# A two-block transformer kernel on one core: order of ScalarE's copies, source of the bias transfers, engine of the softmax scaling, and placement of half projections in its dilated attention

## The reference, cut to what matters

```python
q = rms(h @ w_q) * 64 ** -0.5                      # 3 groups x 16 heads x 64
for g, (window, dil) in enumerate(((128, 1), (512, 4), (2048, 16))):
    s = q_g @ k_g.T + bias_g                       # only distances <= window that dil divides
    ...
    lse = logsumexp(s); p = exp(s - lse); o_g = p @ v_g
wts = softmax(lse over the 3 groups)
o = sum_g wts_g * o_g
x = x + o @ w_o
```

## Time and profile before

| what | us |
|---|---|
| median of 3 runs (lowest to highest) | 2189.49 (2183.22 to 2194.12) |
| the profiled execution, as timed | 2188.71 |
| its span in the trace | 2186.9 |
| of this the dilated block, about | 1758 to 1984 |
| busy over the span: PE, DVE, ACT, POOL | 2013.5, 1170.5, 991.9, 501.5 |

### The profile page before, as it was taken

How to read it: one execution, slowest core, us unless ns; L and a number is a source line. 1 busy time by engine, 2 the same in 40 slices (tenths; PEclk the granted TensorE clock), 3 DMA queues, 4 the chain that set the end, 5 groups by cost and what they waited for, 6 DMA issues and landing times.

```text
span 2186.9 us, 36846 instructions
## 1 busy us (share of the span) xinstructions
PE 2013.5 (92%) x15863; PEld 1925.6 (88%) x15863; DVE 1170.5 (54%) x1389; ACT 991.9 (45%) x1157; POOL 501.5 (23%) x117
## 2 busy tenths in 40 slices
PE   7887999989899979999887999999999987879999
PEld 7875899988799979999886999899899986659998
DVE  5336577665577664437785633433444354556443
ACT  4325344355443453436333533476643455534433
POOL 1100122322022222230330123333222333001322
PEclk9867999999999999999888999999999999979999
DMA  7300345443245525555321455455455544324552
GB/s 263 136 17 1 116 156 192 168 164 135 97 155 193 191 97 193 175 190 183 117 78 58 159 187 173 160 174 167 144 181 189 176 162 151 101 63 151 177 187 102
DMA packets 57313, 321.13 MB, mean 147 GB/s; under 512 B 5693, under 2 KB 19124, under 8 KB 19828
## 3 DMA queue, kind: packets, MB, share of 16 engines
q1 hardware_dynamic: 42644, 304.49, 40.2%
q10 hardware_dynamic: 14560, 15.06, 2.3%
HBM read 318.41 MB, written 1.12 MB: 146 GB/s over the span
## 4 chain that ended last, share of the span: by engine, by line
PE 71%; issue 11%; DVE 10%; ACT 5%; DMA 1%; POOL 1%; ACTq 0%; SPq 0%; DVEq 0%; POOLq 0%
PE bank L371 22%; PE bank L372 22%; PE bank L373 22%; DVE lo L344 3%; ACT hi L338 1%; PE bank L429 1%; DVE xl L829 1%; PE bank L1502 1%; ACT arena L1663 1%; PE bank L466 1%; DMA arena<-rel_rows 1%; DVE arena L1577 1%; DVE arena L505 1%; POOL lo L344 1%; DVE arena L858 1%
## 5 line engine op out<-in xcount | busy, mean ns | idle before, releaser
L371 PE MATMUL bank<-xh,hi 128*128 128x256 f32 x3208 | 924.7, 288 | 37.4 <-DVE xl L829 20.2
L372 PE MATMUL bank<-xl,hi 128*128 128x256 f32 x3208 | 918.0, 286 | 0.0
L373 PE MATMUL bank<-xh,lo 128*128 128x256 f32 x3208 | 917.3, 286 | 0.0
L344 POOL TENSOR_TENSOR lo<-ring,hi 128x2048 fp32r<-128x2048 f32 x97 | 454.2, 4684 | 1548.3 <-ACT hi L338 1548.3
L338 ACT ACTIVATE hi<-ring 128x2048 fp32r<-128x2048 f32 x291 | 550.4, 1899 | 475.7 <-PE bank L373 471.0
L344 DVE TENSOR_TENSOR lo<-ring,hi 128x2048 fp32r<-128x2048 f32 x194 | 509.1, 2625 | 369.1 <-ACT hi L338 368.9
L371 PEld LDWEIGHTS bank<-xh,hi 128*128 128x128 f32 x3208 | 625.1, 195 | 50.4 <-issue 32.6
L372 PEld LDWEIGHTS bank<-xl,hi 128*128 128x128 f32 x3208 | 625.4, 195 | 0.6 <-issue 0.5
L373 PEld LDWEIGHTS bank<-xh,lo 128*128 128x128 f32 x3208 | 625.2, 195 | 0.2
L371 PE MATMUL bank<-gh,hi 128*128 128x256 f32 x1056 | 302.1, 286 | 16.5 <-DVE gl L765 15.7
L372 PE MATMUL bank<-gl,hi 128*128 128x256 f32 x1056 | 301.2, 285 | 0.0
(11 more groups left out here) (264 smaller groups left out, 1810.1 us busy)
## 6 DMA issues: line engine op xcount, KB each, us to landing
ring<-in_ffn_in SPq DMA_DIRECT2D x132, 1024.0 KB, 4.9
ring<-in_ffn_out SPq DMA_DIRECT2D x66, 1024.0 KB, 4.9
ring<-in_kv SPq DMA_DIRECT2D x24, 1024.0 KB, 4.8
ring<-in_hg_in SPq DMA_DIRECT2D x16, 1024.0 KB, 4.8
ring<-in_od_in SPq DMA_DIRECT2D x12, 1024.0 KB, 5.0
ring<-in_dq SPq DMA_DIRECT2D x12, 1024.0 KB, 4.8
ring<-in_ev_in SPq DMA_DIRECT2D x11, 1024.0 KB, 5.0
arena<-rel_rows ACTq DMA_DIRECT2D x16, 384.0 KB, 4.7
```

The source lines that it names most:

```text
L344: ns.tensor_tensor(lo[n % RING][:, 0:w], ring[n % RING][:, 0:w], hi[n % RING][:, 0:w].bitcast(F32), ALU.subtract).then_inc(lo_ok[lo_by[n]], 1)
L371: nc.tensor.matmul(out_, lh, rh, start=start, stop=False, **kw)
L372: nc.tensor.matmul(out_, lh, rl, start=False, stop=False, **kw)
L373: return nc.tensor.matmul(out_, ll, rh, start=False, stop=stop, **kw)
```

## The change

It has five parts, all in the dilated block, or in the helper `Soft` for this block alone:

1. ACT's order in `soft_act`: the hook with `squares` stands behind the copies of the turned blocks, no longer ahead of them.
2. The bias rows are issued by SP, in line with its loads: those of pair 0 behind the load of chunk 4, of pair 1 behind that of chunk 10, of pair 2 behind 11, of 3 behind 13, of 4 behind 14, of 5, 6 and 7 behind 15. Each still waits for the last addition of the unit before it.
3. The scaling of the exponentials is done by GpSimd (`soft_pool`). DVE keeps one reciprocal for each unit, which waits for the exponentials of both heads.
4. In return the low parts of chunks 5 to 11 move from GpSimd to DVE. GpSimd keeps chunks 1 and 3.
5. In rounds 0 to 4 the chunk `inside` is cut in two: its first half stands between the scores of the first and the second group, its second half between those of the second and the third.

```diff
             elif b == "dilated":
-                lo_by += ["V" if c in (0, 2, 4) or c >= 12 else "P" for c in range(len(streams[b]))]
+                lo_by += ["P" if c in (1, 3) else "V" for c in range(len(streams[b]))]
...
+        def scaled(s, u, e):
+            a, rr = s.att[u % s.nr][e], s.rr[:, 2 * (u % 4) + e, :]
+            return [(a[:, :, c0:c1], a[:, :, c0:c1], rr[:, r:r + 1].unsqueeze(2).broadcast_to([P, s.ns, c1 - c0]))
+                    for c0, c1, r in ((0, T, 3), (T, 384, 2))]
+
+        def soft_pool(pool, s):
+            for u in range(len(s.units)):
+                pool.wait_ge(*s.at("rec", u + 1))
+                for e in range(2):
+                    for out, exps, r in scaled(s, u, e):
+                        last = nc.gpsimd.tensor_tensor(out, exps, r, ALU.mult)
+                    last.then_inc(soft_sem["p"], 1)
...
             def weights(u):
...
-                for e in range(2):
-                    if not s.late:
-                        dve.wait_ge(*s.at("exp", 2 * u + e + 1))
-                        rec_step(nc.vector.reciprocal(both[:, e, 2:4], both[:, e, 0:2]))
-                    nc.vector.tensor_tensor(a[e][:, :, 0:T], a[e][:, :, 0:T],
-                                            both[:, e, 3:4].unsqueeze(2).broadcast_to([P, ns, T]), ALU.mult)
-                    nc.vector.tensor_tensor(a[e][:, :, T:384], a[e][:, :, T:384],
-                                            both[:, e, 2:3].unsqueeze(2).broadcast_to([P, ns, P]),
-                                            ALU.mult).then_inc(soft_sem["p"], 1)
+                dve.wait_ge(*s.at("exp", 2 * u + 2))
+                rec_step(nc.vector.reciprocal(both[:, :, 2:4], both[:, :, 0:2]))
...
+                if not s.by_pool:
+                    for e in range(2):
+                        for out, exps, r in scaled(s, u, e):
+                            last = nc.vector.tensor_tensor(out, exps, r, ALU.mult)
+                        last.then_inc(soft_sem["p"], 1)
...
                 if i in s.exps_first and 0 <= u < U:
                     exps(u)
-                s.hook(s.mid, "act", i, act)
+                if s.late:
+                    s.hook(s.mid, "act", i, act)
                 if j >= 0:
                     turned(j)
+                if not s.late:
+                    s.hook(s.mid, "act", i, act)
...
-            def biases_in(act, p):
+            def biases_in(sp, p):
                 if p >= 1:
-                    act.wait_ge(*soft.at("masked", 6 * p))
+                    sp.wait_ge(*soft.at("masked", 6 * p))
+                else:
+                    sp.wait_ge(rel_sent, 16)
+                    sp.wait_ge(lin, 1)
...
+            def sp_after(c):
+
+                return {4: [0], 10: [1], 11: [2], 13: [3], 14: [4], 15: [5, 6, 7]}.get(c, [])
...
-            soft.step = {(i, 2): lambda pe, c=c: project(pe, c) for i, c in inside.items()}
+            soft.step = {(i, h): half(c, h) for i, c in inside.items() for h in range(2)}
...
-            soft.after_exps = {p: lambda act, p=p: biases_in(act, p + 1) for p in range(7)}
...
+                        if b in parts and "sp" in parts[b]:
+                            parts[b]["sp"](sp, c)
```

More of the change, by code:

```diff
@@ L381, in build, with __init__ @@
         class Soft:
-            def __init__(self, units, ns, late, att, pt, nm, rr, copies, held=()):
+            def __init__(self, units, ns, late, att, pt, nm, rr, copies, held=(), by_pool=False):
+                self.by_pool = by_pool
                 self.units, self.ns, self.late, self.att, self.pt, self.nm, self.rr = units, ns, late, att, pt, nm, rr
@@ L389, in __init__ @@
                 self.after = {"pe": {}, "dve": {}, "act": {}}
-                self.turn_after, self.step, self.exps_first, self.after_exps = {}, {}, set(range(len(units) + 1)), {}
+                self.turn_after, self.step, self.exps_first = {}, {}, set(range(len(units) + 1))
                 n, pairs = len(units), 1 + max(un["pair"] for un in units)
@@ L396, in __init__ @@
                 adds = {"qk": n * ns, "masked": 2 * n * ns, "max": 2 * n, "exp": 2 * n,
-                        "rec": n * (1 if late else 2) + gates, "p": 2 * n, "turned": 2 * n * ns, "pt": 2 * n * ns,
+                        "rec": n + gates, "p": 2 * n, "turned": 2 * n * ns, "pt": 2 * n * ns,
                         "pv": n * ns, "oh": pairs - len(held), "o": pairs}
@@ L1914, in make_dilated @@
             N_HELD = 2
-            soft = Soft(units, 3, False, att, pt, NM, RR, copies, [DK[:, p, :] for p in range(N_HELD)])
+            soft = Soft(units, 3, False, att, pt, NM, RR, copies, [DK[:, p, :] for p in range(N_HELD)], True)
             inside = {0: 5, 1: 6, 2: 8, 3: 9, 4: 11}
@@ L1997, in biases_in, with sp_part @@
                         src = bass.AP(tensor=rel_rows.tensor, offset=(2 * p + e) * 1152 + u0, ap=[[1, P], [384, 3], [1, n]])
-                        act.dma_start(REL[e][:, :, lo:lo + n], src).then_inc(rel_in, 16)
+                        sp.dma_start(REL[e][:, :, lo:lo + n], src).then_inc(rel_in, 16)
+            def sp_after(c):
+                return {4: [0], 10: [1], 11: [2], 13: [3], 14: [4], 15: [5, 6, 7]}.get(c, [])
+            def sp_part(sp, c):
+                for p in sp_after(c):
+                    biases_in(sp, p)
             def dve_mid(i):
@@ L2066, in act_part @@
                 soft_act(act, soft)
-            return {"pe": pe_part, "dve": dve_part, "act": act_part}
+            return {"pe": pe_part, "dve": dve_part, "act": act_part, "sp": sp_part, "pool": lambda pool: soft_pool(pool, soft)}
         makers = {"even": make_even, "fox": make_fox, "hgrn": make_hgrn, "kv": make_kv, "dilated": make_dilated}
```

12 lines of the change are left out of this document (3 added, 9 removed).

## The result

The changed kernel takes 2208.05 us (median of 4 runs, 2204.8 to 2210.6), the kernel before 2187.66 us in the runs beside it. The ratio is 1.0081, with a 95% interval from 1.0058 to 1.0105: slower. (It is not the quotient of the two medians, which is 1.0093; so a difference told by ratios and one told by medians can be some 2 us apart.) The profiled execution took 2206.97 us with a span of 2205.2, which is 18.3 more than before. The whole difference stands behind the first scores of the dilated block. From the first scores of round 0 to the first turn of round 5 it was 108.15 us (1796.49 to 1904.64), and is 123.1 (1796.56 to 1919.65): +14.9. From that turn to the end it was 282.3, and is 285.55: +3.3.

What follows compares the result with a forecast made beforehand. PE, on 71% of the chain, was taken as the bound. 7.8 us up to round 5, 6.6 behind it and 5 of clock gave +19.4 on 2188.71, so 2208 us, range 2193 to 2222.

Steps and rivals of the forecast that it cites:

- a chain that was hidden is not any more: In rounds 0 to 4, additions, maxima and exponentials behind the third scores, 5.5 us, no longer run beside the chunk.
- The pause: In rounds 1 to 4 PE idles some 4.3 us in one piece behind the first turn, waiting for ACT's copy.
- Rounds 1 to 4: Rebuilt at 17.9 us each plus means, chunk and waits; against before: -3.7, +2.0, -0.4 and +3.4 us.
- three waits of the prediction: Round 1: 1.5 us for bias rows; round 2: 0.6 for the take-out and 0.5 for squares ahead of the means.
- The clock: Pauses in rounds 0 to 4 bring stretches at the lower clock level: 5 us taken, between none and 8.
- The tail: Behind round 5, turns wait for GpSimd's scaling, 4.5 us a unit against DVE's 3.0: +6.6 us in sum.
- The roots of round 4: Squares, high part and an output copy precede the roots, delaying round 5's turn: round 4 takes 24.1 us, +3.4.
- Bias rows: Pair 1's rows, issued by SP behind chunk 10's load, land around 1822, costing 1.5 us of wait in round 1.
- the faster one: Rival: waits between scores and late copies go, only GpSimd's 6.6 us is new: -12.7, 2176 us; chance 0.09.
- The cheap one: Rival, no change: chain exposed, but no slow stretch, GpSimd 3.0 us a unit, rows land in 4.8: 2197; chance 0.21.
- SP would be the bound: Rival, slower still: bias rows land 9.1 us after issue, scaling costs 5.3, pauses slow the clock: 2221 us; chance 0.14.
- the late copies: In four rounds the second turn waits for ACT's copies behind squares and a high part: 4 x 2.2 us saved.

Runs made afterwards that it cites:

- halves_0_2: Changed kernel with the inner chunk's second half behind the third scores instead of ahead of them; 2187.35 us, ratio to before 0.9988.
- filled: Changed kernel with matmuls whose results are never read put into PE's pauses in rounds 0 to 4; 2198.81 us, ratio to before 1.0052.
- dve_scales: Changed kernel with the scaling of the weights back on DVE; 2201.77 us, ratio to before 1.0063.
- whole_chunks: Changed kernel with the chunks of rounds 0 to 4 in one piece behind the third group's scores; 2188.25 us, ratio to before 1.0001.
- sp_bias_only: Kernel before with only the bias rows issued by SP, by the change's own table of loads; 2187.77 us, ratio to before 0.9995.
- late_on_vector: Changed kernel with whole chunks behind the third scores and units 5 to 7 scaled by DVE; 2183.46 us, ratio to before 0.9965.
- pool_scales_only: Kernel before with only GpSimd's scaling, one reciprocal a unit, and the low parts moved to DVE; 2198.80 us, ratio to before 1.0038.

## Why the prediction was right

It said 2208, in a range from 2193 to 2222, slower; 2208.05 was measured. The mechanism was the one named: a chain that was hidden is not any more. That the number fits to a microsecond is luck. The profiled execution moved by 18.3 us where 19.4 were said, and the terms behind it were off by more than that, in both directions. By its own steps:

- **The pause.** 4.3 us were foretold for rounds 1 to 4, and came as 4.39 three times, 5.19 in round 1. In round 0 the half of chunk 5 was to start near 1799.5 and did at 1799.10, the means near 1814.5 and did at 1814.21. From start to start round 0 took 21.8 us instead of 14.3, +7.5, where +6.5 was said.
- **Rounds 1 to 4.** Foretold 25.2, 21.8, 24.0 and 24.1 us before any clock; measured 26.0, 23.4, 26.75 and 25.1. Together they are 6.2 too long. PE worked at the lower level for 19.6 us in them, which at 44 to 50% is 8.6 to 9.8 us. So without the clock they were some 3 us shorter than foretold, and three waits of the prediction did not come: 1.5 for the bias rows in round 1, and in round 2 the 0.6 for the take-out and the 0.5 for the squares.
- **The clock.** The sum held 5 us for it, with 8 as the most. The slow stretches of rounds 0 to 4 cost 10 to 11 (22.5 us of work at the lower level). That hardly showed in the total, because the sum set rounds rebuilt at full clock against rounds of before that hold 4 us of slow clock themselves (8.6 us of work), and because the tail had less of it than before. Rounds 0 to 4 came out at +14.9; the prediction's 7.8 and 5 make 12.8. From before to after the clock took 6 to 7 us more in the rounds (halves_0_2 and filled point at 6 to 8), and 4 less in the tail. The term was right in kind, and it was the least founded: one stretch in the earlier trace rows, and a guess between none and 8.
- **The tail.** +6.6 was said and +3.3 measured (in dve_scales against the changed kernel it is 4.1 in the traces). 4.5 us a unit was right for units 6 and 7: 4.46, with 1.47 for the larger shape and 0.83 for the smaller. It was not for unit 5 (7.01), where the prediction had not looked at what DVE does beside it. The turns waited 5.70 + 1.31 and 6.56 + 1.31 us for GpSimd, where it had been 3.31 + 0.92 and 4.16 + 0.99 for DVE, 2.8 and 2.7 more; unit 5's 4.62 in place of 0.59 is 4.0 more. The two scores' waits of 1.22 came back. So the waits of PE did grow by 7.1 us, near the term. That the end moved by less is the clock: PE worked 18.5 us at the lower level there, where it had been 27.2 (3.4 of them behind the units, from 1985.9), which is 4 us less lost. The prediction had no such term.
- **The roots of round 4** were to end 5.5 us behind the last product. The turn that waits for them stood 1.53 us, and round 4 took 25.1 for the 24.1.
- **Bias rows.** The addition came at 1821.84, where 1822 was said. But the 1.5 us of wait that the prediction drew from it did not come: PE had no wait for a bank in round 1, and from the first scores to the second turn it took 14.88 us, against 14.74 in round 2. DVE had caught up before the third scores. Their lateness in round 3 did not show, since the exposed chain covers it: it does in whole_chunks.

Of the rivals, the faster one (the waits go and nothing replaces them) died of the point that the prediction named, the maxima that need all three groups. The cheap one (2197) left out 5 us of clock, 4.5 of scaling and 1.5 of bias rows. filled, which takes most of the slow clock out of the rounds and leaves GpSimd's 4.5 us a unit, took 2198.81; so the choice between 2197 and 2208 hung mainly on the clock, the term with the least under it. That SP would be the bound did not come (sp_bias_only: 2187.77 us).

For GpSimd's price the trace decides for the broadcast row: 4.46 us for 2304 elements against DVE's 3.0 is a ratio of 1.5 for this form, with one operand broadcast. An estimate by the 1.96 of the Trainium skill (GPSIMD Engine Reference, section 3.1) would have been 5.9.

What the prediction did not see is that the same change holds one part that gains 0.6% by itself. It priced the late copies (4 x 2.2 us) only as part of a rival, and went on to the sum.

## What to carry to other kernels

Before work is moved in between steps, ask which step the longest chain starts from, and keep that step as early as it was: three scores close together cost 1.3 us of bank waits a round and hid 5.5 us. A change of five parts can hide a good one behind a bad one, so price each alone. A pause of TensorE can cost more than its length where the granted clock falls with it; filling it with dead products tells roughly how much.

## What the runs showed of the hardware

- The granted clock follows the pauses of TensorE: with matmuls that nobody reads in the pauses it went from 0.88 to 0.97, and some 6 us came back, with overlapping intervals. The pauses of 1.3 to 1.5 us in the turns (three in filled, three in halves_0_2) had no slow stretch with them or right behind, each of those of 4.4 us had one, and with pauses of 7 to 8 us the clock was 0.84. In between it goes either way: of the three pauses of 2.17 us in the kernel before, one had a slow stretch. Pauses outside the turns count too: late_on_vector, whose copies came within 0.25 us, had 0.92, with slow stretches at its waits of 3.34 and 4.60 us for the additions and a third one (1865.6) soon behind a wait of 1.49.
- GpSimd and VectorE hold each other up when both read two operands from SBUF: four scalings took 7.01 us instead of 4.46 beside a low part of DVE that kept its 2.29. The Trainium skill (SBUF — State Buffer, section SBUF: two separate sides) says that such operations lock a shared port pair, and the one that comes second waits. Unit 5 agrees: the low part began at 1931.40, 0.05 us ahead of the scaling, and lost nothing, while GpSimd's row is 2.55 us longer. The next operation of DVE, of 512 elements, came second and took 1.95 us; with the scaling on DVE (dve_scales) it took 0.68. In pool_scales_only a low part began at 1830.27, 2.4 us behind a scaling, and took 3.42 us, the scaling 6.51. The rows show the sums, not the order in which the two took turns.
